# A two-layer streaming encoder on one core: prompt heads and sample batches in two separate loops, cache loaded already transposed

## What is computed

```python
D_MODEL, SEQ, DEC_BATCH, DEC_SEQ, PAST_LEN = 1024, 512, 8, 16, 512
H_B, NOPE, ROPE, V_B, Q_LORA, KV_LORA = 8, 128, 64, 128, 384, 256

def expand_kv(ckv, krope, w_uk, w_uv):
    k_nope = (ckv @ w_uk).reshape(B, S, H_B, NOPE)
    k = concatenate([k_nope, broadcast(krope)], -1)
    v = (ckv @ w_uv).reshape(B, S, H_B, V_B)

def mla_layer(x, k, v, ...):
    proj = rmsnorm(x) @ w_in                    # q_lat (384), gate (1024)
    q = (rmsnorm(q_lat) @ w_uq)                 # per head 128 nope + 64 rope
    s = einsum(q, k) * scale                    # block-causal mask for the prompt
    o = einsum(softmax(s), v) * silu(gate)
    return x + rmsnorm(o @ w_out)
```

## Time and profile before

| | us |
|---|---|
| median of 3 runs (lowest, highest) | 748.53 (747.96, 754.56) |
| the profiled execution's own time | 748.36 |
| its span in the profile | 746.6 |
| TensorE busy (share of span) | 668.5 (90%) |
| VectorE busy | 444.0 (59%) |
| ScalarE busy | 294.9 (39%) |
| GpSimd busy | 178.8 (24%) |

### The profile page before, as it was taken

The page is one execution under the profiler, slowest core; times in us unless marked ns, Lnnn a source line. Parts: engine busy times, 40 slices in busy tenths (PEclk is TensorE's granted clock), DMA queues, the critical chain, the costliest instruction groups (busy, mean ns, idle before and its releaser), DMA issues.

```text
span 746.6 us, 12627 instructions
## 1 busy us (share of the span) xinstructions
PE 668.5 (90%) x4954; PEld 632.7 (85%) x4954; DVE 444.0 (59%) x651; ACT 294.9 (39%) x564; POOL 178.8 (24%) x179
## 2 busy tenths in 40 slices
PE   2796897999999977998899999989989999978995
PEld 1666896999999967997899989988878787878995
DVE  4416328467558566226765767536778878785324
ACT  5264423233234133235422422644465565544221
POOL 4500104306117034116342410320202122110004
PEclk9788998999999989999899999898999999999999
DMA  9302303613425254213123410433221111207103
GB/s 305 91 0 58 101 13 104 185 56 112 125 64 169 57 176 142 57 58 137 68 79 88 134 36 6 138 105 100 61 60 60 45 31 58 64 2 278 34 1 141
DMA packets 73261, 67.19 MB, mean 90 GB/s; under 512 B 13154, under 2 KB 69730, under 8 KB 73075
## 3 DMA queue, kind: packets, MB, share of 16 engines
q1 hardware_dynamic: 73202, 66.39, 28.8%
HBM read 55.60 MB, written 10.78 MB: 89 GB/s over the span
## 4 chain that ended last, share of the span: by engine, by line
PE 61%; DVE 22%; ACT 8%; issue 5%; POOL 2%; DMA 0%; SPq 0%; DVEq 0%; ACTq 0%; POOLq 0%
PE bank L1265 19%; PE bank L1266 19%; PE bank L1267 19%; DVE slab_lo L979 4%; DVE pT_lo L979 2%; ACT prob L937 1%; DVE oT_lo L979 1%; DVE hat_lo L979 1%; PE bank L1305 1%; DVE sT_lo L979 1%; ACT slab_hi L767 1%; DVE stat L1241 1%; DVE kN_lo L979 1%; DVE stat L1215 1%; PE bank L1457 1%
## 5 line engine op out<-in xcount | busy, mean ns | idle before, releaser
L1265 PE MATMUL bank<-slab_hi,hat_hi 128*128 128x256 f32 (+1 forms) x600 | 173.4, 289 | 15.1 <-DVE hat_lo L979 10.0
L1266 PE MATMUL bank<-slab_lo,hat_hi 128*128 128x256 f32 (+1 forms) x600 | 171.5, 286 | 0.0
L1267 PE MATMUL bank<-slab_hi,hat_lo 128*128 128x256 f32 (+1 forms) x600 | 171.2, 285 | 0.0
L1265 PEld LDWEIGHTS bank<-slab_hi,hat_hi 128*128 128x128 f32 x600 | 118.3, 197 | 17.6 <-DVE hat_lo L979 10.6
L1266 PEld LDWEIGHTS bank<-slab_lo,hat_hi 128*128 128x128 f32 x600 | 118.6, 198 | 0.0
L1267 PEld LDWEIGHTS bank<-slab_hi,hat_lo 128*128 128x128 f32 x600 | 118.4, 197 | 0.0
L979 DVE TENSOR_TENSOR slab_lo<-stage,slab_hi 128x1024 fp32r<-128x1024 f32 (+4 forms) x75 | 91.0, 1213 | 18.5 <-ACT slab_hi L767 16.1
L1265 PE MATMUL bank<-hat_hi,slab_hi 128*128 128x320 f32 (+1 forms) x272 | 86.0, 316 | 1.3 <-DVE slab_lo L979 0.9
L767 ACT ACTIVATE slab_hi<-stage 128x1024 fp32r<-128x1024 f32 (+4 forms) x75 | 74.5, 994 | 28.6 <-issue 14.5
L1266 PE MATMUL bank<-hat_lo,slab_hi 128*128 128x320 f32 (+1 forms) x272 | 85.0, 313 | 0.0
L1267 PE MATMUL bank<-hat_hi,slab_lo 128*128 128x320 f32 (+1 forms) x272 | 84.8, 312 | 0.0
(11 more groups left out here) (320 smaller groups left out, 1598.1 us busy)
## 6 DMA issues: line engine op xcount, KB each, us to landing
stage<-in_a_w_in_dram SPq DMA_DIRECT2D x24, 512.0 KB, 4.7
stage<-in_b_w_in_dram SPq DMA_DIRECT2D x10, 512.0 KB, 4.2
st_s<-in_state_gla_dram SPq DMA_DIRECT2D x4, 1024.0 KB, 6.5
out_dram<-st_s SPq DMA_DIRECT2D x4, 1024.0 KB, 5.2
stage<-in_a_w_out_dram SPq DMA_DIRECT2D x8, 512.0 KB, 4.6
craw<-in_cache_ckv_dram SPq DMA_DIRECT2D x8, 512.0 KB, 4.6
stage<-in_b_w_out_dram SPq DMA_DIRECT2D x8, 512.0 KB, 4.5
stage<-in_b_w_uq_dram SPq DMA_DIRECT2D x16, 192.0 KB, 2.7
```

Of the source, the lines that this page charges most:

```text
L1265: pe.matmul(out, a[0], b[0], start=first, stop=False)
L1266: pe.matmul(out, a[0], b[1], start=False, stop=False)
L1267: return pe.matmul(out, a[1], b[0], start=False, stop=last)
```

## The change

1. The host passes three more arrays: the cached latents transposed (`ckvT`), the rotary keys transposed (`kropeT`) and the key weights transposed (`w_ukT`). `ct`, `cr` and `wt` have no TensorE part any more. SP loads `sT_raw` (`ldT`, 512 KB), `sk_raw` (`ldR`, twice 128 KB) and `craw` (`ldN`, 512 KB, in place of `ldc`). ScalarE makes the `_hi` of each; VectorE makes `sT_lo` (`ct`), GpSimd makes `skL` (`cr`) and `cn_lo` (`cs`).
2. `cs` was GpSimd's alone (copy and subtraction); now ScalarE copies and GpSimd subtracts. The raw buffers share memory with the `_lo` buffers.
3. The `pre` slabs and `qns` go: `qn` now computes the 512 prompt and 128 sample columns of a head in one (2 x 320 columns), and `qabs` runs per head.
4. All values (`vh`) are computed in the lead-in, in 8 steps of 512 columns, and kept for all heads; the slabs `uvn` hold their weights. A `hd` slab has 896 columns as before, with `w_ukT` in place of w_uv.
5. One loop over the prompt heads, then one over the samples. `y`,B,0 becomes four steps `y0`, spread over the samples.
6. In stage A, `y` and `ys` wait for `oT` tile by tile, and the load of slab `wo`,A,1 stands behind the last `oT`. Memory is laid out anew.

The probabilities are scaled on VectorE (`N`) in both kernels. The core of the diff:

```diff
+    out += [("vh", 0, t) for t in range(NP)] + [("vh", 1, 0), ("vh", 1, 1)]
+    load(("hd", 2))
+    out += [("qn", 0), ("kh", 0), ("vh", 1, 2), ("vh", 1, 3), ("qabs", 0)]
+    load(("hd", 3))
+    prompt_heads(out, load)
+    samples(out, load)
+
+def prompt_heads(out, load):
+    for h in range(-1, HB):
+        if h >= 0:
+            out += [("T", h, 0), ("T", h, 1)]
+        if h + 1 < HB:
+            out += [("S", h + 1, 0), ("S", h + 1, 1), ("N", h + 1, 0), ("N", h + 1, 1)]
         if h + 2 < HB:
+            out += [("qn", h + 2), ("kh", h + 2)]
+        if h >= 0 and h + 4 < HB:
+            load(("hd", h + 4))
+        if h == 4:
             load(("wo", "B", 0))
+        if h == HB - 2:
+            out += [("ct", 0), ("cr", 0), ("ldR", 1), ("ldN", 1)]
+            load("uv")
+        if h == HB - 1:
+            out += [("ct", 1), ("cr", 1), ("ss", 1), ("ldT", 3), ("ldR", 3)]
+        if h >= 0:
+            out += [("O", h), ("Oh", h)]
         if h + 2 < HB:
+            out += [("qabs", h + 2)]
+        if h == 4:
+            out += [("ldT", 0), ("ldR", 0), ("ldN", 0)]
+        if h == HB - 3:
+            out += [("ldT", 1)]
+        if h == HB - 2:
+            out += [("ss", 0), ("ldT", 2), ("ldR", 2), ("cs", 0)]
+
+def samples(out, load):
+    out += [("cs", 1)]
+    for b in range(SB):
+        out += [("st", b)]
+        if b + 2 < SB:
+            out += [("ct", b + 2), ("cr", b + 2), ("ss", b + 2)]
+            if b + 4 < SB:
+                out += [("ldT", b + 4), ("ldR", b + 4)]
+        if b in (1, 3):
+            out += [("y0", b // 2)]
+        if b:
+            out += [("cx", b - 1)]
+        if b == SB - 1:
+            load(("wo", "B", 1))
+            out += [("y0", 2)]
+        out += [("sv", b)]
+        if b + 2 < SB:
+            out += [("ldN", b + 2), ("cs", b + 2)]
+    out += [("ldk",), ("y0", 3), ("cx", SB - 1)]
...
-    "cr": ("pe", "act", "dve"), "ss": ("pe", "dve", "act"), "cs": ("pool",),
+    "cr": ("act", "pool"), "ss": ("pe", "dve", "act"), "cs": ("act", "pool"),
...
+        sT_raw = [put(block_at[(4, 1)[i]], f"sT_raw{i}", [P, KC, PAST]) for i in range(2)]
+        cn_hi = [put(block_at[(7, 3)[i]], f"cn_hi{i}", [P, PAST // P, KL], fp32r) for i in range(2)]
+        cn_lo = [put((block_at[6], kN_at)[i], f"cn_lo{i}", [P, PAST // P, KL], fp32r) for i in range(2)]
+        craw = [put((block_at[6], kN_at)[i], f"craw{i}", [P, PAST // P, KL]) for i in range(2)]
...
+                elif kind == "ldT":
+                    b = step[1]
+                    after(sp, "pe", *(("ss", b - 2) if b > 1 else ("O", (4, 5)[b])))
+                    sp.dma_start(sT_raw[b % 2][:, :, :], dram["ckvT"][b]).then_inc(turned_in[b % 2], 16)
+                elif kind == "ldN":
+                    b = step[1]
+                    after(sp, "pe", *(("sv", b - 2) if b > 1 else ("S", HB - 1, 1) if b else ("O", 4)))
                     sp.dma_start(craw[b % 2][:, :, :], dram["cache_ckv"][b]...).then_inc(cache_in[b % 2], 16)
...
                 elif kind == "ct":
-                    last = copy(sT[0][:, :, :], bank[:, :, :])
+                    b = step[1]
+                    act.wait_ge(turned_in[b % 2], 16 * (b // 2 + 1))
+                    if b == 1:
+                        after(act, "pe", "O", 6)
+                    last = copy(sT_hi[b % 2][:, :, :], sT_raw[b % 2][:, :, :])
+                elif kind == "cs":
+                    b = step[1]
+                    act.wait_ge(cache_in[b % 2], 16 * (b // 2 + 1))
+                    if b == 1:
+                        after(act, "pe", "O", HB - 1)
+                    last = copy(cn_hi[b % 2][:, :, :], craw[b % 2][:, :, :])
...
                 elif kind == "cs":
+                    after(pool, "act", *step)
-                    pool.wait_ge(cache_in[b % 2], 32 * (b // 2 + 1))
-                    after(pool, "pe", *(("sv", b - 1) if b else ("gb", 0, 1)))
-                    link(pool.tensor_copy(cn[0][:, :, :], craw[b % 2][:, :, :]))
-                    last = pool.tensor_tensor(cn[1][:, :, :], craw[b % 2][:, :, :], raw(cn[0][:, :, :]), SUB)
+                    last = pool.tensor_tensor(cn_lo[b % 2][:, :, :], craw[b % 2][:, :, :], raw(cn_hi[b % 2][:, :, :]), SUB)
...
                 elif kind == "ss":
                     b = step[1]
-                    after(pe, "dve", "cr", b)
-                    after(pe, "dve", "qabs", HB // 2 - 1)
+                    after(pe, "dve", "ct", b)
+                    after(pe, "pool", "cr", b)
+                    after(pe, "dve", "qabs", HB - 1)
```

More of the change, by code:

```diff
@@ L153, in steps @@
                 out += [("gl", t), ("oT", t - EARLY_GATE)]
+            out += [("oT", t) for t in range(NT - EARLY_GATE, NT)]
             load(("wo", "A", 1))
-            out += [("oT", t) for t in range(NT - EARLY_GATE, NT)]
         else:
@@ L202, in latent_layer @@
     load(("gb", 2))
-    out += [("gb", 3, 0), ("cT", 0), ("cT", 1), ("gb", 3, 1), ("cT", 2), ("cT", 3), ("cT", 4)]
+    out += [("gb", 3, 0)] + [("cT", t) for t in range(NT)] + [("gb", 3, 1)]
     load("uqr")
@@ L206, in latent_layer @@
     load(("gb", 1))
[L207 to L211, removed]
+    out += [("qr", 0), ("qr", 1), ("qr", 2), ("qrT", 0), ("gb", 1, 0), ("qrT", 1), ("qr", 3), ("qrT", 2), ("qr", 4)]
     load(("gb", 0))
-    out += [("qrT", 4), ("qabs", 0), ("qns", 1), ("wt", 1)]
-    load(("pre", 2))
-    out += [("gb", 0, 0), ("qabs", 1), ("qns", 2), ("wt", 2), ("ldc", 0), ("ldc", 1), ("gb", 0, 1)]
@@ L216, in latent_layer @@
-    load(("pre", 3))
+    out += [("gb", 1, 1), ("qrT", 3)]
+    load(("uvn", 0))
+    load(("uvn", 1))
+    out += [("gb", 0, 0), ("qrT", 4), ("gb", 0, 1)]
     load(("hd", 0))
-    out += [("qabs", 2), ("ct", 0), ("cr", 0), ("qns", 3), ("wt", 3)]
     load(("hd", 1))
[L220 to L234, removed]
-        if h + 2 < HB:
[L236 to L241, removed]
-            load(("wo", "B", 0))
-        out += [("O", h), ("Oh", h)]
-        if not more:
-            out += [("sv", h)]
-        if h + 2 < HB:
[L247 to L250, removed]
@@ L321 @@
 for _s in range(4):
-    USERS["gb", _s], USERS["pre", _s] = ("gb", _s, 1), ("wt", _s)
+    USERS["gb", _s] = ("gb", _s, 1)
 for _h in range(HB):
-    USERS["hd", _h] = ("kh", _h) if _h % 2 else ("vh", _h // 2)
+    USERS["hd", _h] = ("qabs", _h)
+for _g in range(2):
+    USERS["uvn", _g] = ("vh", _g, NP - 1)
 STAT = {}
@@ L500, in program @@
-        place[0] = gate_at
-        kraw = [sb(f"kraw{i}", [P, PAST // P, ROPE]) for i in range(2)]
+        place[0] = temp_at
+        spT = pair("spT", [P, TOK])
+        place[0] = prob_at
+        sprob.append(sb("sprob1", [P, NT, P]))
+        place[0] = gate_at
+        qN_at = place[0]
+        qN = pair("qN", [P, TOK])
+        kN_at = place[0]
+        kN = pair("kN", [P, SEQ])
+        vN_at = place[0]
+        vN = sb("vN", [P, HB, 2, NP, VB], fp32r)
+        assert place[0] <= phase_at
@@ L1124, in _ @@
                                 else dve.tensor_scalar(v, o, S1(("o", h), stat2, t), None, MUL))
+                elif kind == "y0":
+                    t = step[1]
+                    dve.wait_ge(post_in, 48)
+                    last = tt(y_rows[:, t, 0:256], bank[:, 0, 0:256], post[:, 0:256], MUL)
                 elif kind in ("y", "ys"):
@@ L1200, in _ @@
                 elif kind == "qn":
-                    last = low(qN[1][:, :], bank[:, 0, :], qN[0][:, :])
-                elif kind == "qns":
-                    last = low(qN_s[1][:, :], bank[:, 0, 0:2 * P], qN_s[0][:, :])
+                    hi, lo = (x[:, :].rearrange("p (a n) -> p a n", a=2) for x in qN)
+                    last = low(lo, bank[:, :, 0:HALF], hi)
                 elif kind == "kh":
@@ L1391, in _ @@
                     ready(("wo", ph, s))
-                    after(pe, "dve", *(("oT", NP - 1 if kind == "y" else NP) if ph == "A" else ("Oh", HB - 2)))
                     last = natural(row, ("wo", ph, s), range(NP) if kind == "y" else [NP], 256, KD, hat if ph == "A" else None)
+                elif kind == "y0":
+                    t = step[1]
+                    ready(("wo", "B", 0))
+                    after(pe, "dve", "Oh", HB - 1)
+                    last = natural(row, ("wo", "B", 0), [t], 256, KD, None)
                 elif kind == "yt":
@@ L1542, in _ @@
                     for s in range(NT):
-                        last = mm3(bank[:, 0, 0:KL], cut(spT, A_, slice(s * P, (s + 1) * P)), cut(cn, A_, s) if s < NT - 1 else cut(cn_s, A_, A_), s == 0, s == NT - 1)
+                        last = mm3(bank[:, 0, 0:KL], cut(spT, A_, slice(s * P, (s + 1) * P)), cut((cn_hi[b % 2], cn_lo[b % 2]), A_, s) if s < NT - 1 else cut(cn_s, A_, A_), s == 0, s == NT - 1)
                 elif kind == "cx":
```

238 lines of the change are left out of this document (117 added, 121 removed), and 1 row of the table PARTS.

## The result

The changed kernel takes 800.22 us (median of 4 runs, 799.75 to 800.87), the kernel before, measured beside it, 748.82 us (747.96 to 754.56). The ratio is 1.067, with a 95% interval of 1.062 to 1.072. The forecast was 797 us, in a range of 768 to 822.

What follows compares the result with a forecast made beforehand. It took TensorE to bound all but the end before, and a closed loop through a load to stall the samples after. 61 + 111 + 127.6 = 299.6 against 250.2: 748.4 + 49.4, about 797 us, range 768 to 822.

Steps and rivals of the forecast that it cites:

- Lead-in, 61: Stretch up to the first `S`: 76.5 us before, forecast 61, bounds 59 and 67, with 2.6 for handoffs.
- Heads, 111: Loop over prompt heads without samples: 12.2 us a head, 8.2 for head -1, 25 for the end; 111 us.
- D: Rival for the heads: VectorE and ScalarE bind them at 14 us each, +11, total 808; chance 0.06.
- Samples, 127.6: From the end of O 7 up to `so`: turns of 18.0 us stalled behind a load; 127.6 us in all.
- The collision: In the samples, GpSimd's `cs` subtraction delays VectorE's `ct`; ScalarE's `ct` to end of `cr` 2.5 us, bounds 1.9 and 3.1.
- Half clock 2.4 a turn: In the samples, TensorE runs at 1.2 GHz after standing some 9 us; costs 2.4 us a turn.
- B: Rival for samples: no half clock worth naming, no collision, load 4.0 to 4.6, turn 14 to 15.5, total 778; chance 0.16.
- C: Rival for samples: all of a turn at 1.2 GHz, loads at 6.1, full collision; 22 a turn, total 821; chance 0.08.
- Rival A: Samples are bound by TensorE, because ScalarE's copy finds its values landed; total 724; chance 0.06.
- A sign that failed: In some 100 us before `so`, TensorE under 45% busy, with granted clock well below 1.
- The step that failed: Opening claim on where the change acts: 438.8 to 678.1 us, and `y`,B,0 just behind, to 689.0.
- my ring: Samples' closed loop: load after `sv` b, ScalarE's `cs`, `ct` b+3, `ss` b+3, then `sv` b+1; 18.0 us a turn.

Runs made afterwards that it cites:

- the transposes: Changed kernel plus 72 transposes of an identity on TensorE before each `ss` from 2 on; 799.86 us, ratio 1.067.

## Why the prediction was right

The total came within 3.2 us because each of its three stretches did, within 1.2 us; it missed 4.5 us ahead of them. Some of that closeness is luck: the 4.5 are 7.8 lost less 3.3 gained, neither of them forecast, and inside the heads errors of 1 to 2 us cancel.

- **Lead-in, 61:** 59.8 measured. TensorE was busy 59.05, where my items add up to 58.2 (I wrote 58.4), and idle 0.75, so the 2.6 for handoffs was too much.
- **Heads, 111:** 111.7. Heads 0 to 5 took 71.2 us for 73.2: three of them 11.6 us each, the others 11.3, 11.9 and 13.1. I took a middle between TensorE's 11.7 and a guess of friction; in the head shown there was none, for VectorE is busy 9.9 and not 11.2. Head -1 took 9.4 for 8.2, and the end 26.4 for 25. Small errors that cancel. D (14 a head) is out.
- **Samples, 127.6:** 126.6. By terms: load 5.2 forecast, 3.8 to 4.9 measured; ScalarE 3.0, measured 2.9; from ScalarE's `ct` to the end of `cr` 2.5, measured 2.9; TensorE with the half clock 7.3, measured 7.1. The load was overpriced, since I priced it as one close behind 768 KB of other transfers. Two of the first five were issued so, 2 us behind them, and took 4.9 and 4.4 us; the others took 3.8 to 3.9.
- **The collision:** GpSimd's `skL` took 2.07 us beside VectorE, and 1.12 of it after VectorE had ended, about the 1.2 that I gave the whole operation. I had left open whether GpSimd is held up; it is. By the exclusive lock of the Trainium skill, page SBUF — State Buffer, section "SBUF: two separate sides", that term was 3.1; the trace agrees with the rule, and 3.1 was nearer to the 2.9 than my value. That no run showed GpSimd as the loser was wrong: in the trace of the kernel before, an operation of GpSimd that takes 0.83 us at its shortest took 1.16 beside VectorE's 2.03 of the earlier trace rows, which had started first and ended at 580.31:

```profile
579.84 1.16 POOL L721 TENSOR_TENSOR stage<-stage,gain_b_q_norm 128x384 f32<-128x384 f32 x1
```

- **Half clock 2.4 a turn:** the transposes took 2.1 away. So B (no half clock, no collision) fails on both conditions, and C (all of the turn at it, loads of 6.1) is not reached.
- **Rival A** is out, and its break-even of 9.8 us a turn was wrong by the prediction's own sum: it lets six turns shrink from 18 us, and the sum has the sixth, up to `sv` 6, at 10.7. By that sum it is (89 + 10.7 - 49.4) / 6 = 8.4 us, without `y0`. (B's 6 x 3.2 has the same slip.) With `ct` ahead alone the six turns average 8.7 without their `y0`, and the kernel was still 1.6% slower; 4.5 us of that are the ones ahead.
- **A sign that failed:** I said TensorE would be under 45% busy there; it was 50% (63.5 of 126.6 us). Work at 1.2 GHz counts as busy for up to twice as long (`so`'s matmuls take 5.6 us at full clock and took 9.1 with most of them at 1.2 GHz). The sign should have been written in work, not in busy time.
- **The step that failed:** "The change touches 438.8 to 678.1 us" put all that lies ahead of 438.8 at nothing, and was wrong at two places of which I worked out neither. Stage A gained 3.3 by the end of `gb` 3,0, `cT`'s order lost 7.8. I had not looked up which bank `cT` 3 reuses, and who reads it.

The mechanism was right but incomplete, and the total could not have told. In my ring `ss` b+3 needs `ct` b+3, and `ct` stands behind `cs`, which waits for the load. True, and the sum of its links gave the time. But I took the load for the cause. Without it a turn is still 14 us, since `ct` stands behind the last exponentials too. That stands in no row of before, yet the printed order of steps has it: `ss` b+2, with its exponentials on ScalarE, stands right ahead of `ct` b+3 of the next turn. I read it there only after an experiment had opened one ring and left the other.

## What to carry to other kernels

When a turn's time equals the sum of its links, that shows a closed ring, not which link to cut: write each engine's in-order list of one turn down and look for every edge that leads from the end of `ss` back to its own input. Of two rings that share links only the longer one shows, so an edit that opens one can look like a failure (17 to 14 us, and still slower than before) and be a third of the remedy (21.8 of 59.5 us). Put what prepares the next turn's matmuls ahead of this turn's exponentials on ScalarE, and what reads a fresh load as far behind its issue as the buffers let it. And where an order is only "moved", ask which bank or buffer the next step reuses, and who still has to read it.

## What the runs showed of the hardware

Stretches at 1.2 GHz came with every idle time of 9 to 10 us on TensorE. In most turns such a stretch took 10.2 us, 13.6 and 17.1 us were seen too, and it began while TensorE still stood. Filling the idle time kept the clock at full speed there. A stretch of 10.2 us on `so`, with TensorE busy all through it, was seen in that kernel and in the one without the load, and cost 4.7 us each time. Which work gets a longer stretch differs between the kernels; single turns and `so` moved by 1.7 to 4.7 us with it, and the cause of that stays open. GpSimd's subtraction of 512 columns ended 1.12 us after VectorE's, whether VectorE took 1.23 us or 1.65.
